# Row pitch of the split activations (264 to 288 columns) and a shifted common zone in a hybrid decoder kernel

## The reference

```
h = x + 1/2 * post(SwiGLU_1(pre(x)))
h = h + post(W_out( sum_i sigmoid(gate_i) * W_branch_i(branch_i(pre(h))) ))
h = h + 1/2 * post(SwiGLU_2(pre(h)))
rms_norm(x, g) = x * rsqrt(mean(x*x) + 1e-6) * g          # pre, post and the memory norm
swiglu(x)      = (silu(gate) * up) @ w_out,  [gate, up] = x @ w_in     # 1024 -> 2*2816 -> 1024
branch 0: retention, 4 heads, key 128, value 256, decay per head, chunked recurrence with state
branch 1: gated delta rule with a causal convolution of 4 taps on q/k/v, 4 heads, state
branch 2: attention of 4 heads (256 wide) into 256 memory tokens, k and v = rms_norm(mem) @ w_mem
w_in: 1024 -> 10248 columns (q, k, v, gates of the branches), w_branch and w_out: 1024 -> 1024
```

## Time and profile before

| | |
|---|---|
| median of 3 runs | 1829.15 us (1828.1 to 1831.79) |
| profiled execution | 1834.74 us, of which the span of instructions 1832.9 us |
| granted TensorE clock | mean 0.997 of full speed |
| TensorE matmul | busy 1788.5 us (98%), 16247 instructions |
| TensorE weight load | busy 1726.6 us (94%) |
| VectorE | busy 1306.6 us (71%) |
| ScalarE | busy 885.6 us (48%) |
| GpSimd | busy 139.8 us (8%) |
| DMA | 376.65 MB, mean 205 GB/s |

### The profile page before, as it was taken

How to read it: one execution, slowest core, us unless ns; L and a number is a source line. 1 busy time by engine, 2 the same in 40 slices (tenths; PEclk the granted TensorE clock), 3 DMA queues, 4 the chain that set the end, 5 groups by cost and what they waited for, 6 DMA issues and landing times.

```text
span 1832.9 us, 40342 instructions
## 1 busy us (share of the span) xinstructions
PE 1788.5 (98%) x16247; PEld 1726.6 (94%) x16247; DVE 1306.6 (71%) x2065; ACT 885.6 (48%) x1038; POOL 139.8 (8%) x214
## 2 busy tenths in 40 slices
PE   6999999999999999999999999999999999999998
PEld 6999999988899999999999999998889899999998
DVE  6677566787777877777567765768786776877754
ACT  5443354546574254543364434554466635354333
POOL 0000002211210100000000000031112010000000
PEclk9999999999999999999999999999999999999999
DMA  7876657967875656666667766697778565546654
GB/s 230 220 206 192 182 187 233 321 209 229 269 234 164 215 179 214 171 189 170 175 194 216 209 185 196 191 293 246 232 240 278 177 213 172 180 138 193 180 162 135
DMA packets 436433, 376.65 MB, mean 205 GB/s; under 512 B 10098, under 2 KB 411892, under 8 KB 435626
## 3 DMA queue, kind: packets, MB, share of 16 engines
q1 hardware_dynamic: 409560, 276.60, 50.7%
q0 software_dynamic: 26688, 97.48, 15.9%
HBM read 347.29 MB, written 26.76 MB: 204 GB/s over the span
## 4 chain that ended last, share of the span: by engine, by line
PE 72%; DVE 11%; DMA 8%; issue 5%; ACT 4%; POOL 0%; DVEq 0%; SPq 0%; ACTq 0%; POOLq 0%
PE proj L716 48%; PE proj L734 5%; PE proj L739 5%; PE proj L735 4%; DMA raw<-w_in 3%; DVE wl L1892 3%; PE proj L690 2%; ACT wh L1400 2%; DMA queries<-qrow 2%; PE aux L928 1%; DMA qsp<-queries 1%; DVE sring L2329 1%; PE aux L1097 1%; PE aux L781 1%; DMA raw<-w_mem_v 1%
## 5 line engine op out<-in xcount | busy, mean ns | idle before, releaser
L1892 DVE TENSOR_TENSOR wl<-raw,wh 128x2048 fp32r<-128x2048 f32 (+1 forms) x280 | 599.2, 2140 | 195.4 <-ACT wh L1400 172.3
L1400 ACT CAST wh<-raw 128x2048 fp32r<-128x2048 f32 (+1 forms) x280 | 500.3, 1787 | 273.8 <-PE proj L716 118.1
L716 PE MATMUL proj<-xh,wh 128*128 128x264 f32 x2624 | 384.5, 289 | 0.4 <-ACT wh L1400 0.3
L716 PE MATMUL proj<-xl,wh 128*128 128x264 f32 x2624 | 381.8, 286 | 0.0
L716 PE MATMUL proj<-xh,wl 128*128 128x264 f32 x2624 | 371.5, 284 | 2.6 <-DVE wl L1892 2.5
L716 PEld LDWEIGHTS proj<-xl,wh 128*128 128x128 f32 x2624 | 342.1, 189 | 12.9 <-issue 12.3
L716 PEld LDWEIGHTS proj<-xh,wh 128*128 128x128 f32 x2624 | 342.3, 189 | 3.8 <-issue 0.8
L716 PEld LDWEIGHTS proj<-xh,wl 128*128 128x128 f32 x2624 | 338.7, 188 | 4.4 <-DVE wl L1892 4.3
L734 PE MATMUL proj<-hh,wh 128*128 128x264 f32 x704 | 173.7, 284 | 0.0
L735 PE MATMUL proj<-hl,wh 128*128 128x264 f32 x704 | 173.4, 283 | 0.0
L1421 ACT ACTIVATE gate<-gate 128x264 f32<-128x264 f32 x88 | 37.4, 425 | 242.8 <-DVEq L1927 242.8
(11 more groups left out here) (477 smaller groups left out, 2200.7 us busy)
## 6 DMA issues: line engine op xcount, KB each, us to landing
raw<-ffn_w_in SPq DMA_DIRECT2D x176, 512.0 KB, 5.2
raw<-w_in SPq DMA_DIRECT2D x80, 1024.0 KB, 6.1
raw<-ffn_w_out SPq DMA_DIRECT2D x64, 704.0 KB, 4.6
sring<-cache_mem_k POOLq DMA_DIRECT2D x32, 512.0 KB, 6.5
sring<-cache_mem_v POOLq DMA_DIRECT2D x32, 512.0 KB, 4.9
out<-sring POOLq DMA_DIRECT2D x32, 512.0 KB, 4.2
sring<-state_gdn POOLq DMA_DIRECT2D x30, 512.0 KB, 5.3
raw<-w_mem_v SPq DMA_DIRECT2D x8, 1024.0 KB, 7.8
```

The costliest lines, as they stand in the source:

```text
L716: mm = pe.matmul(o, w[:, s, k * 256 + t * P:k * 256 + (t + 1) * P], a[:, k, :], **go)
L1400: act.copy(wh[:, slot, 0:size], raw[:, slot, 0:size]).then_inc(hi_done[slot], 1)
L1892: dve.tensor_sub(wl[:, slot, 0:size], raw[:, slot, 0:size], wh[:, slot, 0:size].bitcast(F32)).then_inc(split_done[slot], 1)
```

## The change

`xh` and `xl` get rows of 288 columns (1152 bytes, nine times 128), of which the first 264 are used as before. Their starts stay at 128 above a multiple of 256 (`xh` at byte 12,672 as before, `xl` at 21,888), so the rows' starts alternate between 128 above a multiple of 256 and a multiple of 256. The 24 columns left at the end of each row hold the small tables: `gains` (14) and `gl` (7) beside `xh`, `rds` (8) and `rsv` (8) beside `xl`. Everything from `y` to `csum` moves up by 1536 bytes, a multiple of 256. A filler of 24 columns ahead of the common zone brings its start to byte 137,216, a multiple of 256; offsets inside the zone are as before. Rows of `hh`, `hl`, `oh`, `ol`, `ohd`, `old`, `mh` and `ml` stay 264 columns apart.

Every engine has the same instructions in the same order. What differs is the addresses, and the form of the few that touch several rows at once: line 1543's `128x1056` becomes `128x4x264` (line 2072's too), and the copies of the small tables get one more dimension.

```diff
+TW = 288
-        xh, xl = sb("xh", [P, KT, T], F32R), sb("xl", [P, KT, T], F32R)
+        def beside(name):
+            with ExitStack() as own:
+                rest = own.enter_context(nc.sbuf_tensor(name + "_beside", [P, KT, TW], F32))
+            return sb(name, [P, KT, TW], F32R)[:, :, 0:T], rest
+
+        (xh, xhw), (xl, xlw) = beside("xh"), beside("xl")
+        gains, gl = xhw[:, :, T:T + 14], xhw[:, :, T + 14:T + 21]
+        rds, rsv = xlw[:, :, T:T + NS], xlw[:, :, T + NS:T + 2 * NS]
-        gains, gl = sb("gains", [P, KT, 14]), sb("gl", [P, KT, 7])
-        rds, rsv = sb("rds", [P, KT, NS]), sb("rsv", [P, KT, NS])
+        sb("zone_start", [P, 24])
         ZONE = 91776
```

## The result

The changed kernel takes 1838.38 us (median of 4 executions, 1837.45 to 1839.4), the kernel before beside it 1829.32 us (4 executions). The recorded ratio is 1.0034 with the interval 1.0017 to 1.005: 3 to 9 us slower. (The plain quotient of these two medians is 1.0050, at the upper end of that interval.) The forecast was 1827.5 us in a range of 1800 to 1834, so the time lies outside. Both intervals exclude no change, and together they speak for a loss of 3 to 5 us.

A forecast was written before the change was run, and what follows sets the result against it. TensorE's start-to-start distance per matmul was taken to bound the kernel. Rows 0, memory zone -1.5, `vst` -0.2 and small tables 0 gave -1.7 us from the median 1829.15: 1827.5 us, range 1800 to 1834.

The forecast's parts named there:

- Bound and leverage: TensorE's cost per matmul sets the kernel's time; 8096 matmuls read `xh` or `xl`, so 1 ns each is 8.1 us.
- (a): `wabr` matmuls, 40 weight columns, stream rows at all eight places at an even 121 ns: row start shows no cost.
- The count of pieces: A 264-column row touches equally many 32- to 256-byte pieces from any multiple of 32, so `xh` and `xl` gain 0.
- the prediction's last guess: If the first SwiGLU's 1008-matmul piece fell over 0.5 us: row place costs with long weight loads, hidden by short ones.
- (b): In the SwiGLU stage, with 128 weight columns, durations spread from 278 to 289 ns, but the mean distance stays 121 ns.
- (c): With 256 columns there are two speeds, 113.3 and 117.8 ns, and the start alone does not decide which.
- The zone, -1.5 and -0.2: Better-placed `memh` and `meml` speed up 384 matmuls, -1.5 us; `vst` as moving operand of 128 matmuls, -0.2 us.
- Small tables and forms: Table copies and reads on ScalarE and VectorE cost the same from new addresses: +0.0 us, first `gains` copy bounded at 0.1.
- Rival B: Fixed pitch locks `xh` and `xl` rows into a slow rhythm, up to 4.5 ns each: 1864 us at full weight; chance 0.12.
- Rival A: Rows at multiples of 128 bytes, weights at 128, run at 116.6 ns: 1796 to 1812 us, middle 1804; chance 0.38.
- the fast rhythm: The faster 256-column speed, 113.3 ns, plus 3.3 for 8 more columns: 116.6 ns per matmul, 4.3 less.
- The bounds of the term: For the 8096 matmuls on `xh` and `xl` rows: gain 34.8 us at 4.3 ns each, loss 36 us at 4.5 ns.

The follow-up runs named there:

- unpadded_moved_64: The kernel before with `xh` and `xl` 64 bytes later, pitch still 1056: 1833.02 us against 1831.99, ratio 1.0003 (0.9991 to 1.0015).
- bare_matmuls: Separate kernel computing nothing of the reference, 45 blocks of 96 matmuls on TensorE alone; 264 columns from 128: 120.83 ns at pitch 1056, 121.67 at 1152.
- zone_only: The kernel before with only the common zone moved to a multiple of 256: 1833.1 us, ratio 0.9999 (0.999 to 1.0009).
- the fast version: The changed kernel with `wh` and `wl` 64 bytes later: 1813.03 us against 1831.99 of before, ratio 0.9894 (0.9868 to 0.992).
- place_map: Separate kernel of bare matmuls, pitch and start stepped by 32 bytes, weights at 128; 264 columns at pitch 1152: 116.65 to 123.4 ns by start.
- pitch_only: The changed kernel with the common zone back at 64 above a multiple of 256: 1836.63 us against 1832.46, ratio 1.002 (1.0012 to 1.0029).

## Why the prediction was wrong

- **Bound and leverage: right.** TensorE's distance from start to start is the time, 8096 matmuls hang on it, 1 ns is 8.1 us at most. Most of the loss shows (6.5 us by the matmuls, 6.7 of busy time, 4.2 of span); a gain in the mixer does not.
- **The step that failed: "From (a) and this count I take 0 for the rows of `xh` and `xl`."** It measured +0.8 ns each. The count of pieces looked at the moving row alone. The bare matmuls show that the row's place against the weights sets the distance from start to start, and not its own start.
- **Why reading (a) misled.** The earlier trace rows have moving rows at all eight places, and they really are even: 120 to 121 ns from start to start within each run. But the weights there are steps of 160 bytes (40 columns), so x minus w grows by 1056 - 160 = 896 bytes per row, which is 128 modulo 256: the pair takes two relative places, not eight. In the changed kernel `wabr` has moved too, from 160 to 0, and x minus w grows by 1152 - 160 = 992, 224 modulo 256, and takes all eight; there the same matmuls stand 117 to 126 ns apart, as the durations of 278 to 285 above hint. So the very rows that seemed to rule the place out turned uneven when places changed, and the prediction's last guess, that a short weight load hides the place, is wrong too. The two relative places are not the whole reason for the even rows. In unpadded_moved_64 the pair takes two as well (the rows 64 bytes on, `wabr` still at 160), and the distances run from 117 to 123 ns; in bare_matmuls the block L120 has just the pitches and starts of the earlier trace rows, and its distances run from 116 to 123 ns. That the earlier trace rows came out even was no proof of anything general; why they did is open.
- **Why (b) was the better row.** The spread of the earlier trace rows with the full weights said that rows and weights act together., of which (c) speaks, are another matter: `wh` and `wl` both start at 128, so `memh` meets them at the same place modulo 256, and still takes 117.8 ns with `wh` and 114.5 with `wl` from start to start. That is the second thing, besides the place, which the last section lists. The prediction wrote "the start alone does not decide" and then let it decide.
- **The zone, -1.5 and -0.2: wrong in sign, too small to see.** Line 714 and the memory keys became slower, and `vst` (the -0.2) did not become faster, with 120 ns as its usual distance in place of 118; zone_only measures 0.9999.
- **Small tables and forms, 0: right,** VectorE and ScalarE within 0.5 us. What the ends of rows cost inside one instruction had been shown by no run; the remainders that now write four separate rows take 1255 ns for 1254, so nothing that shows.
- **Rival B, with 0.12, is what happened, in its small size.** A fixed pitch locked the rows into two places, 0.8 ns dearer than the drift and above the 0.67 at which it was to decide. Its upper bound of 4.5 ns was not met at any place of pitch 1152; the worst is 123.4, 2.5 above the drift.
- **Rival A, with 0.38, has a true mechanism and the wrong place.** The prediction worked out 116.6 ns for the fast rhythm, and 116.67 is what the runs show. It put it at rows and weights both at 128; it needs 64 between them. So the price of the fast rhythm was read rightly, and the reason given for it (rows at a multiple of 128 bytes) was not: those rows take 121.67 ns. Its range end of 1800 came from this, and the fast version lands at 1813.
- **The range** should have been as wide above as below. The bounds of the term were -34.8 and +36 us, and the range took in nearly all of one and 4.85 us of the other.

## What to carry to other kernels

Where TensorE sets the time, look at the place of the moving rows relative to the weights, not at either alone, and read distances from start to start in sums over a whole run of rows; durations overlap and mislead. At the drifting pitch of 1056 bytes the start does not matter (120.83 to 120.85 ns from all eight); at the fixed pitch of 1152 it decides between 116.7, 121.7 and 123.3 ns: fixing the pitch without choosing the offset is a draw of lots. A kernel of bare matmuls with a few dozen blocks gives the table in one run, and its figures for 264 columns at these two pitches held in the kernel to 0.4 ns. Blocks should be repeated, since one place gave two speeds, and the figures for 256 columns did not carry over.

## What the runs showed of the hardware

- Float32r matmuls of 264 columns and 128 weight columns take 116.65 to 126.67 ns from start to start at a granted clock of 1.0 and with no other engine at work, 116.7 to 123.4 ns by the start alone at pitch 1152; 256 columns take 113.3 to 120.0 ns. 110.0 and 106.7 would be the columns at 2.4 GHz.
- At a pitch of 1280, every row at one place, the distance goes by x minus w, within 0.1 ns, for the four differences (128, -64, 0, 64) that were tried from two or three starts. At 96 the same start gave 121.67 ns once and 126.67 ns once (bare_matmuls L105, place_map L147). The pitch counts besides: at x minus w = 128, 1280 gives 123.33 ns and 2048 gives 120.0. With 256 columns at pitch 1024: -64 takes 113.3 ns, 64 takes 117.8, 128 takes 118.7, 0 takes 120.0.
- The table does not carry over everywhere. In the kernel before line 714 runs at 113.4 ns with differences of 64 and -64 in turn, and the memory keys (the same two differences) at 117.0 to 118.1 ns; the table has 113.3 for one difference and 117.8 for the other in both. In pitch_only line 714 changes from about 117.5 to 113.4 ns within one stretch, at the same places. With 264 columns too: three of its four output stages of the SwiGLU take 64.41 us from the first start to the last, and one 63.97 us, for the same 528 matmuls at the same places. So a second thing besides the place sets the rhythm; what it is was not tried.
- What inside the chip makes the difference count was not shown. The runs exclude other engines' traffic (none ran) and that it matters whether the weights are new or the same again (11.60 us for 96 matmuls either way).
